# Odd layer's values taken head by head beside their queries and keys, its gates later, and a signal for every 256 columns of a weight's low part

## The chip, the cores and the metric

One Trainium2 chip, one of its NeuronCores. The metric is the device time of one execution of the whole program in microseconds (us). The work is in float32: the two operands of every large product are each split into a high part that TensorE takes in its fast format and a low remainder, and a product is three passes (high by high, low by high, high by low).

## What is computed

Two small transformer blocks one after the other, on 512 tokens of 1024 features. The first has an "even" layer (sliding-window and chunked attention) and an "odd" layer (differential attention). The second has a state-space mixer, a latent attention and two feed-forward networks. The change touches the odd layer and the splitting of all weights. The odd layer is, cut:

```python
h = rms_norm(x, norm_g)
q, k, v, gate = jnp.split(h @ w_in, [C_QK, 2 * C_QK, 2 * C_QK + C_W], axis=-1)   # 4 x 1024 columns
q = rms_norm(q.reshape(b, s, C_HEADS, 2, HEAD_DIM), qn)                # 8 heads, 2 x 64 each
k = rms_norm(k.reshape(b, s, C_HEADS, 2, HEAD_DIM), kn)
q1, q2, k1, k2 = ...                                                   # rope on each half
v = v.reshape(b, s, C_HEADS, C_V_DIM)                                  # 8 heads of 128
o = differential_attention(q1, q2, k1, k2, v, lam)                     # softmax 1 - lam * softmax 2, times v
o = rms_norm(o, subln_g) * (1.0 - lambda_init)
y = (o.reshape(b, s, C_W) * jax.nn.silu(gate)) @ w_out
return x + y
```

## The kernel before, in words

**Tiles.** Activations lie feature by feature: 8 tiles of 128 features by 512 tokens, each as a high and a low copy (`xh`, `xl`). A weight is a piece of 128 x 1024 numbers (512 KB, eight 128 x 128 blocks). For each one SP loads it into one of three `stage` buffers, ACT copies it into `wh` (step `w_hi`, one instruction, L2005), POOL subtracts that from the original into `wl` (step `w_lo`, four instructions of 256 columns, L2569, of which only the last signals), and TensorE (PE) multiplies: step `mm` is one block by all 512 tokens in three passes (L1839, L1840, and L1842, which takes the low part of the weight and waits for `w_lo` of the whole weight), eight steps to an output tile. `mm_half` (L1851, L1852, L1854) is the same for 256 tokens, `mm_tok` (L1864, L1866, L1867) gives an output with tokens on the partitions. There are three `wh`/`wl` pairs, so a weight can only be split once the third weight before it is used up.

**The order of the work.** A planner (`Plan`) runs generators against lengths of its own for each step (`length`, `LENGTHS`) and writes down a fixed order of instructions for each engine. At each moment it takes the step that can start first, and of those the one of the lowest rank. Attention has rank 1 and 2, the preparation of queries and keys 4, and the stream of projections 8, so the stream fills what attention leaves of PE. On the chip the order is fixed: an instruction that is not ready holds up all behind it on its engine.

**Odd layer before.** `stream` projects: the gates 0 to 2 by halves while the norm is still being finished (`proj_border_g`), gate 3, queries and keys of head 0, then all values in two batches of four weights (`proj_tok_g`, four PSUM banks each, copied out by DVE in `v_in`, L2232), then for head 1 to 7 its queries and keys, with gates 4 to 7 beside heads 5, 6 and 7 (`Gates.beside`), then the output projection (`outputs`). The first four gates are one ACT instruction each (`gate`, Silu, L2030) between two table loads. The last four are copied out (`gate_in`, L2065) and their Silu is taken in pairs between two table loads (`gate_s`, L2069; the load is L2000). `prep` waits until gates 0 to 3 are done before it starts `qk_prep_g`: square on ACT (L2040), sums over heads on PE (`blk`, L1878, two matmul instructions), ln and exp on ACT, the scaling on DVE (L2259, it frees the projection's bank), a turn of partitions by DMA, two products on POOL (L2577, L2582), a sum on DVE (L2264), and the split into high and low (L2202, L2539). `attend` waits until all eight pieces of values are there. It then takes the heads in order, and in each four blocks of 128 queries one after the other: scores on PE (L1884), mask and minimum on DVE (L2268, L2278), two exps on ACT (L2045), reciprocal, factor and difference on DVE (L2359, L2363, L2367). Each block is then transposed on PE (`flip`, L1892), copied out (L2054 or L2294) and multiplied with the values (`pv`, L1899). `finish` normalises a head (L2060, L2307), turns it back on PE (`feat`, L1906), multiplies it with its gate (L2317) and splits it (L2011, L2227).

**Even layer.** It has one tile of values that is already taken in the new way: copied from PSUM by ACT (`va_in`, L2035), four transposes on PE (`va_t`, L1913), copied by DVE (`va_out`).

Of the kernel before, what the change touches and what calls it, by code (L numbers as in the profile page):

```python
# [8 lines left out]
F32 = mybir.dt.float32  # L9
# [82 lines left out]
PE_DEEP, DMA_DEEP, HOP, OVERLAP = 165, 2200, 36, 90  # L92
HALF = (slice(0, 256), slice(256, 512))
# [49 lines left out]
class Weight:  # L143
# [6 lines left out]
    lo: tuple = None  # L150
    used: tuple = None
    over: bool = False

# [32 lines left out]
class Plan:  # L186
# [46 lines left out]
    def ready(self, kind, o):  # L233
        if kind in ("mm", "mm_half", "mm_tok"):
            x, kk = (o[4], o[5]) if kind == "mm_tok" else (o[3], o[4])
            done = x.half[o[5]] if kind == "mm_half" else x.t
            return max(self.when([done[kk]]), self.when(o[1]), self.when(o[0].bank.freed))
        return self.when(list(o)) + HOP

    def length(self, kind, o):  # L240
        n = o[-1] if o and isinstance(o[-1], int) else 0
        if kind in ("w_hi", "w_lo"):
            return 210 + 0.82 * o[0].n if kind == "w_hi" else 100 + 2.25 * o[0].n
# [116 lines left out]
    def split_weight(self, m):  # L360
# [6 lines left out]
        w.lo = self.put("w_lo", w)  # L367
# [744 lines left out]
def odd_layer(P, x, rt, parts, freed, over):  # L1112
# [4 lines left out]
    gates = Gates(P, mem["o_sg"], over)  # L1117
    v = mem["o_v"]
    tv = []
# [14 lines left out]
    def prep(h, j, gain, key, pool):  # L1134
        u = yield from P.proj_g(x, [w[j]])
        while None in gates.t[0:4]:
            yield lambda: None not in gates.t[0:4]
        P.start(4, P.qk_prep_g(u, (P.V(gain), tgain), True, key, pool,
                               lambda dst: got.setdefault(h, {}).__setitem__(key, dst)))
        return u  # L1140

    def v_post(b, half, u):
        t = yield ("v_in", v[:, b, half * 512:(half + 1) * 512], u, over)
        u.bank.release(t)
        tv.append(t)

    def stream():
        yield from P.proj_border_g(x, [w[j] for j in range(3)], lambda j, u: P.start(4, gates.first(j, u)))
        P.start(4, gates.first(3, (yield from P.proj_g(x, [w[3]]))))
        yield from prep(0, 8, "od_qn", "q", qs)  # L1150
        yield from prep(0, 16, "od_kn", "k", ks)
        for half in range(2):
            us = []
            for r in (P.at, P.at, P.at, P.ob):
                us.append(Unit((yield from P.taken(r))))
            yield from P.proj_tok_g(x, [T["o_v"][half, j] for j in range(4)], us)
            for b in range(4):
                P.start(5, v_post(b, half, us[b]))
        for h in range(1, 8):
            yield from prep(h, 8 + h, "od_qn", "q", qs)  # L1160
            u = yield from prep(h, 16 + h, "od_kn", "k", ks)
# [32 lines left out]
    def back(h, i, g, ready, ob, mn, sm, rr, to):  # L1194
# [3 lines left out]
        t = yield ("pv", ob, i * 128, 128, [pt.ready, tv], [cols(pt.ap, b) for b in range(nb)],  # L1198
# [6 lines left out]
    def attend():  # L1205
        while len(tv) < 8:
            yield lambda: len(tv) == 8
# [1644 lines left out]
```

## Time and profile before

| | us |
|---|---|
| median of 3 runs | 2012.36 (2011.19 to 2012.7) |
| the profiled execution | 2011.72 |
| its span, first to last instruction | 2009.9 |
| PE busy | 1936.9 (96%) |
| DVE busy | 1042.4 (52%) |
| ACT busy | 990.9 (49%) |
| POOL busy | 946.4 (47%) |

The profiled execution is 0.6 us under the median of the runs and 1.8 us longer than its span. Matmuls overlap: an L1839 row of 0.39 us starts 0.23 us before the next one, and its share of PE's time is the 0.23 us. "Idle before" is time in which an engine did nothing ahead of an instruction, with what ended it. A busy share of 96% means 73 us in which PE did nothing.

### The profile page before, as it was taken

What the parts mean: (1) busy time and instruction counts of PE and PEld (TensorE: products, weight loads), DVE (VectorE), ACT (ScalarE), POOL (GpSimd) and SP (SyncE); (2) the same over time, 40 slices, a digit from 0 to 9 for tenths busy, and PEclk for the clock granted to TensorE, in tenths of its full rate; (3) what the DMA queues carried; (4) which work ended last, traced back from release to release, by engine and by line L of the source; (5) the groups of instructions that cost most, each with busy time, mean ns of one, the idle gap of its engine ahead of it and who ended that gap; (6) DMA issues with size and microseconds to landing.
All of it is one profiled execution on the core that took longest, in us unless ns stands there. A gap on an engine that the chain in (4) does not pass through costs nothing.

```text
span 2009.9 us, 26575 instructions
## 1 busy us (share of the span) xinstructions
PE 1936.9 (96%) x10008; PEld 1607.4 (80%) x10008; DVE 1042.4 (52%) x1934; ACT 990.9 (49%) x1737; POOL 946.4 (47%) x1236
## 2 busy tenths in 40 slices
PE   6999999989989999999999999999999999999997
PEld 5778888866778877777788888888878888888886
DVE  4366543378743677766736564412546574444214
ACT  5466634367743565556526444422555464444323
POOL 4542355554535444444364555555452445555553
PEclk9999999999999999999999999999999999999999
DMA  5321223331222222222132223233221223223332
GB/s 186 95 69 43 61 76 95 90 89 53 84 62 86 74 74 74 75 74 82 56 105 85 100 95 102 94 92 99 77 70 55 74 74 105 95 95 97 95 95 71
DMA packets 55200, 169.36 MB, mean 84 GB/s; under 512 B 7072, under 2 KB 13856, under 8 KB 54944
## 3 DMA queue, kind: packets, MB, share of 16 engines
q1 hardware_dynamic: 54784, 166.92, 26.5%
q8 instruction: 79, 1.29, 0.3%
q10 hardware_dynamic: 288, 0.74, 0.1%
q14 instruction: 49, 0.40, 0.1%
HBM read 158.72 MB, written 2.10 MB: 80 GB/s over the span
## 4 chain that ended last, share of the span: by engine, by line
PE 77%; DVE 12%; ACT 4%; POOL 3%; issue 2%; DMA 1%; SPq 0%; ACTq 0%; DVEq 0%; POOLq 0%
PE ps L1839 19%; PE ps L1842 19%; PE ps L1840 19%; PE ps L1899 2%; POOL wl L2569 2%; PE ps L1851 2%; PE ps L1854 2%; PE ps L1852 2%; PE ps L1884 2%; DVE tmp L2392 1%; PE ps L1892 1%; DVE s_xbc L2371 1%; PE ps L1864 1%; PE ps L1866 1%; PE ps L1867 1%
## 5 line engine op out<-in xcount | busy, mean ns | idle before, releaser
L2569 POOL TENSOR_TENSOR wl<-st,wh 128x256 fp32r<-128x256 f32 (+1 forms) x1180 | 877.2, 776 | 998.7 <-ACT wh L2005 998.2
L2005 ACT ACTIVATE wh<-st 128x1024 fp32r<-128x1024 f32 (+2 forms) x311 | 314.2, 1011 | 502.2 <-PE ps L1842 441.7
L1839 PE MATMUL ps<-xh,wh 128*128 128x512 f32 x1368 | 555.5, 406 | 1.6 <-DVE tmp L2259 1.6
L1842 PE MATMUL ps<-xh,wl 128*128 128x512 f32 x1368 | 534.3, 391 | 0.8 <-POOL wl L2569 0.8
L1840 PE MATMUL ps<-xl,wh 128*128 128x512 f32 x1368 | 533.2, 390 | 0.0
L1839 PEld LDWEIGHTS ps<-xh,wh 128*128 128x128 f32 x1368 | 257.3, 188 | 60.0 <-issue 8.3
L1842 PEld LDWEIGHTS ps<-xh,wl 128*128 128x128 f32 x1368 | 256.7, 188 | 56.9 <-POOL wl L2569 1.7
L1840 PEld LDWEIGHTS ps<-xl,wh 128*128 128x128 f32 x1368 | 257.5, 188 | 49.8 <-issue 2.6
L2526 DVE SCALAR_TENSOR_TENSOR tmp<-ps,vec,tmp 128x510 f32<-128x510 f32 (+1 forms) x176 | 131.3, 749 | 209.8 <-ACT tmp L2184 206.9
L2484 DVE SCALAR_TENSOR_TENSOR res<-res,ps 128x512 f32<-128x512 f32 (+1 forms) x37 | 22.7, 615 | 220.9 <-PE ps L1842 212.2
L1839 PE MATMUL ps<-fa_h,wh 128*128 128x512 f32 x308 | 120.6, 392 | 0.0
L1842 PE MATMUL ps<-fa_h,wl 128*128 128x512 f32 x308 | 119.9, 389 | 0.0
L1840 PE MATMUL ps<-fa_l,wh 128*128 128x512 f32 x308 | 119.8, 389 | 0.0
L1851 PE MATMUL ps<-xh,wh 128*128 128x256 f32 x288 | 86.4, 300 | 8.0 <-DVE xl L2227 5.2
L1854 PE MATMUL ps<-xh,wl 128*128 128x256 f32 x288 | 83.8, 291 | 5.7 <-POOL wl L2569 5.6
L2011 ACT ACTIVATE fa_h<-tmp 128x512 fp32r<-128x512 f32 x44 | 27.8, 632 | 116.8 <-DVE tmp L2532 116.8
L1852 PE MATMUL ps<-xl,wh 128*128 128x256 f32 x288 | 83.5, 290 | 0.0
L2371 DVE SCALAR_TENSOR_TENSOR s_xbc<-ps,vec,s_xbc 128x509 f32<-128x509 f32 (+2 forms) x96 | 71.2, 742 | 9.0 <-ACT s_xbc L2078 8.1
L2045 ACT ACTIVATE o_pr<-ps,small 128x256 f32<-128x256 f32 (+3 forms) x112 | 55.6, 501 | 28.5 <-DVE small L2278 22.2
L1840 PEld LDWEIGHTS ps<-fa_l,wh 128*128 128x128 f32 x308 | 57.8, 188 | 12.5 <-issue 0.5
L1839 PEld LDWEIGHTS ps<-fa_h,wh 128*128 128x128 f32 x308 | 57.8, 188 | 12.4 <-issue 0.5
L1842 PEld LDWEIGHTS ps<-fa_h,wl 128*128 128x128 f32 x308 | 57.8, 188 | 12.0
(276 smaller groups left out, 3508.7 us busy)
## 6 DMA issues: line engine op xcount, KB each, us to landing
st<-in_f_up SPq DMA_DIRECT2D x88, 512.0 KB, 3.2
st<-in_s_xbc SPq DMA_DIRECT2D x32, 512.0 KB, 3.5
st<-in_f_dn SPq DMA_DIRECT2D x32, 512.0 KB, 3.5
st<-in_o_fm SPq DMA_DIRECT2D x24, 512.0 KB, 3.5
st<-in_e_fm SPq DMA_DIRECT2D x21, 512.0 KB, 3.5
st<-in_s_z SPq DMA_DIRECT2D x16, 512.0 KB, 3.5
st<-in_s_out SPq DMA_DIRECT2D x16, 512.0 KB, 3.5
tmp<-tmp SPq DMA_DIRECT2D x100, 64.0 KB, 2.0
```

What stands on the lines that cost most here:

```text
L1839: e.matmul(u.bank.ap, hi, x.h[:, kk, :], start=first, stop=False)
L1840: e.matmul(u.bank.ap, hi, x.l[:, kk, :], start=False, stop=False)
L1842: e.matmul(u.bank.ap, lo, x.h[:, kk, :], start=False, stop=last).then_inc(S["mm"], 1)
L1851: e.matmul(out, hi, x.h[:, kk, part], start=first, stop=False, skip_group_check=True)
L1852: e.matmul(out, hi, x.l[:, kk, part], start=False, stop=False, skip_group_check=True)
L1854: e.matmul(out, lo, x.h[:, kk, part], start=False, stop=last, skip_group_check=True).then_inc(S["mm_half"], 1)
L1884: t = e.matmul(out, q[:, i * 128:i * 128 + 128], k[:, kb0 * 128:kb0 * 128 + n], start=(j == 0), stop=(j == len(passes) - 1))
L2005: e.activation(P.mem["wh"][w.m % NWR][:, 0:w.n], P.mem["stage"][w.m % NSTAGE][:, 0:w.n], ACT.Copy).then_inc(S["w_hi"], 1)
L2045: e.activation(p, s, ACT.Exp, bias=least, scale=-1.0, accum_out=total).then_inc(S["exp"], 1)
L2371: e.scalar_tensor_tensor(v[:, sh:], u.bank.ap[:, 0:SEQ - sh], weight, v[:, sh:], ALU.mult, ALU.add).then_inc(S["tap"], 1)
L2526: e.scalar_tensor_tensor(a.ap[:, sh:], u.bank.ap[:, 0:SEQ - sh], weight, a.ap[:, sh:], ALU.mult, ALU.add).then_inc(S["ftap"], 1)
L2569: t = e.tensor_tensor(P.mem["wl"][w.m % NWR][:, part], P.mem["stage"][w.m % NSTAGE][:, part], P.mem["wh"][w.m % NWR][:, part].bitcast(F32) ...
```

## The change

Four things, in the order of the diff. The low part of a weight is planned and signalled in pieces of 256 columns (`LOW`), each a step of its own, and a matmul waits for the pieces that its block lies in (`Weight.low`): blocks 0 and 1 for the first, 2 and 3 for the second and so on. The planner's length for it goes from 2404 ns for a whole weight to four times 713 ns. In the odd layer the border takes queries, keys and values of head 0, no longer three gates, and `prep` no longer waits for gates. Each head's values are a projection of their own behind its keys, brought into place by `va_in`, `va_t` and `va_out`, and `attend` waits for the values of its own head alone. The gates are all beside heads: two beside head 1, two beside 3, one beside 5, one beside 6, two beside 7, all by `gate_in` and `gate_s`. The layout of the value weights on the host follows.

```diff
+LOW = 256
@@ class Weight
+    def low(self, k, n=128):
+        return self.lo[k * n // LOW:(k * n + n - 1) // LOW + 1]
@@ Plan.ready
-            return max(self.when([done[kk]]), self.when(o[1]), self.when(o[0].bank.freed))
+            low = o[1].low(o[2], o[3]) if kind == "mm_tok" else o[1].low(o[2])
+            return max(self.when([done[kk]]), self.when([o[1].hi, low]), self.when(o[0].bank.freed))
@@ Plan.length
-            return 210 + 0.82 * o[0].n if kind == "w_hi" else 100 + 2.25 * o[0].n
+            return 210 + 0.82 * o[0].n if kind == "w_hi" else 150 + 2.2 * (o[1].stop - o[1].start)
@@ Plan.split_weight
-        w.lo = self.put("w_lo", w)
+        w.lo = [self.put("w_lo", w, slice(at, min(at + LOW, w.n))) for at in range(0, w.n, LOW)]
@@ odd_layer
+    gates.beside = {1: [0, 1], 3: [2, 3], 5: [4], 6: [5], 7: [6, 7]}
-    tv = []
+    tv = [None] * 8
-    def prep(h, j, gain, key, pool):
-        u = yield from P.proj_g(x, [w[j]])
-        while None in gates.t[0:4]:
-            yield lambda: None not in gates.t[0:4]
+    def prep(h, key, u):
+        gain, pool = ("od_qn", qs) if key == "q" else ("od_kn", ks)
         P.start(4, P.qk_prep_g(u, (P.V(gain), tgain), True, key, pool,
                                lambda dst: got.setdefault(h, {}).__setitem__(key, dst)))
-    def v_post(b, half, u):
-        t = yield ("v_in", v[:, b, half * 512:(half + 1) * 512], u, over)
+    def v_post(h, u):
+        vf = yield from P.taken(P.tmp)
+        t = yield ("va_in", vf, u)
         u.bank.release(t)
-        tv.append(t)
+        bank = yield from P.taken(P.aux)
+        t = yield ("va_t", bank, vf, t)
+        vf.release(t)
+        tv[h] = yield ("va_out", v[:, :, h * 128:(h + 1) * 128], bank, [t, over])
+        bank.release(tv[h])
+    def first(j, u):
+        if j < 2:
+            prep(0, "qk"[j], u)
+        else:
+            P.start(4, v_post(0, u))
     def stream():
-        yield from P.proj_border_g(x, [w[j] for j in range(3)], lambda j, u: P.start(4, gates.first(j, u)))
-        P.start(4, gates.first(3, (yield from P.proj_g(x, [w[3]]))))
-        yield from prep(0, 8, "od_qn", "q", qs)
-        yield from prep(0, 16, "od_kn", "k", ks)
-        for half in range(2):
-            ...
-            yield from P.proj_tok_g(x, [T["o_v"][half, j] for j in range(4)], us)
-            for b in range(4):
-                P.start(5, v_post(b, half, us[b]))
+        yield from P.proj_border_g(x, [w[8], w[16], w[24]], first)
         for h in range(1, 8):
-            yield from prep(h, 8 + h, "od_qn", "q", qs)
-            u = yield from prep(h, 16 + h, "od_kn", "k", ks)
+            prep(h, "q", (yield from P.proj_g(x, [w[8 + h]])))
+            prep(h, "k", (yield from P.proj_g(x, [w[16 + h]])))
+            P.start(4, v_post(h, (yield from P.proj_g(x, [w[24 + h]]))))
             for j in gates.beside.get(h, ()):
                 u = yield from P.proj_g(x, [w[j]])
                 P.start(5, gates.bring(j, u))
@@ odd_layer back, attend
-        t = yield ("pv", ob, i * 128, 128, [pt.ready, tv], ...
+        t = yield ("pv", ob, i * 128, 128, [pt.ready, tv[h]], ...
-        while len(tv) < 8:
-            yield lambda: len(tv) == 8
-            while len(got.get(h, ())) < 2:
+            while len(got.get(h, ())) < 2 or tv[h] is None:
@@ pe_program, mm, mm_half and (with n) mm_tok
-            pe.wait_ge(w.lo)
+            pe.wait_ge(w.low(k))
@@ pool_program
-            w, = o
+            w, part = o
             pool.wait_ge(w.hi)
-            for at in range(0, w.n, 256):
-                part = slice(at, min(at + 256, w.n))
-                t = e.tensor_tensor(...)
-            t.then_inc(S["w_lo"], 1)
+            e.tensor_tensor(...).then_inc(S["w_lo"], 1)
```

## Rows read from the trace of the kernel before

**Rows 1.** The page: busy time, and PE and its clock in 40 slices.
```profile
PE 1936.9 (96%) x10008; PEld 1607.4 (80%) x10008; DVE 1042.4 (52%) x1934; ACT 990.9 (49%) x1737; POOL 946.4 (47%) x1236
PE   6999999989989999999999999999999999999997
PEclk9999999999999999999999999999999999999999
```
**Rows 2.** Busy time in stretches of the odd layer, engine by engine.
```profile
core 0: us, PE busy (x) PEld busy (x) DVE busy (x) ACT busy (x) POOL busy (x), PEclk, DMA share, GB/s
318.00:380.20 62.20, 62.20 (x273) 50.76 (x272) 13.37 (x16) 21.76 (x27) 38.40 (x51) 1.00 0.36 112
380.20:397.50 17.30, 16.99 (x85) 13.41 (x83) 9.59 (x23) 9.56 (x24) 6.92 (x9) 1.00 0.33 100
440.00:461.00 21.00, 19.52 (x102) 15.25 (x102) 16.02 (x34) 15.21 (x42) 9.72 (x12) 1.00 0.23 70
557.00:575.50 18.50, 17.35 (x91) 14.24 (x89) 10.21 (x27) 12.12 (x34) 2.83 (x4) 1.00 0.15 56
575.50:590.30 14.80, 10.77 (x46) 8.16 (x45) 5.90 (x10) 7.23 (x18) 3.31 (x5) 0.88 0.00 1
320.00:580.00 260.00, 243.42 (x1175) 190.99 (x1174) 152.26 (x288) 155.20 (x365) 133.11 (x152) 1.00 0.27 80
```
**Rows 3.** Waits of PE, 395 to 582 us: line, for whom, total, times, longest.
```profile
PE ps L1892 <- DVE o_pr L2367: 9.3, 15, 1.9
PE ps L1899 <- DVE o_pt L2294: 2.0, 3, 1.0
PE ps L1899 <- ACT o_pt L2054: 1.7, 2, 1.1
PE ps L1839 <- DVE tmp L2259: 1.6, 2, 1.1
PE ps L1884 <- DVE kz L2539: 1.4, 1, 1.4
PE ps L1906 <- DVE tmp L2307: 0.5, 2, 0.3
```
**Rows 4.** Timeline of PE at heads 0, 1, 6 and 7: start, duration.
```profile
380.19 0.56 PE L1884 MATMUL ps<-kz,qz 128*128 128x128 f32 x4
397.51 0.66 PE L1892 MATMUL ps<-const,o_pr 128*128 128x128 f32 x4 [0.32 <-DVE o_pr L2367]
...
405.55 1.08 PE L1878 MATMUL ps<-tmp,const 128*128 128x512 f32 x2
417.94 0.63 PE L1884 MATMUL ps<-kz,qz 128*128 128x128 f32 x4 [1.35 <-DVE kz L2539]
...
554.20 0.66 PE L1892 MATMUL ps<-const,o_pr 128*128 128x128 f32 x4 [1.93 <-DVE o_pr L2367]
554.61 0.47 PE L1839 MATMUL ps<-xh,wh 128*128 128x512 f32 x1
575.53 0.66 PE L1892 MATMUL ps<-const,o_pr 128*128 128x128 f32 x4
```
**Rows 5.** Waits of PE for the low part of a weight, whole span.
```profile
PE ps L1854 <- POOL wl L2569: 5.6, 3, 2.3
PE ps L1842 <- POOL wl L2569: 2.5, 3, 1.6
```
**Rows 6.** Timeline at one such wait: POOL's four pieces, PE's matmuls.
```profile
17.66 3.54 POOL L2569 TENSOR_TENSOR wl<-st,wh 128x256 fp32r<-128x256 f32 x4 [1.46 <-ACT wh L2005]
...
18.53 0.41 PE L1852 MATMUL ps<-xl,wh 128*128 128x256 f32 x1
21.25 0.58 PE L1854 MATMUL ps<-xh,wl 128*128 128x256 f32 x1 [2.31 <-POOL wl L2569]
```
**Rows 7.** Timeline of PE at the end of the odd layer's attention.
```profile
584.28 0.62 PE L1839 MATMUL ps<-yh,wh 128*128 128x512 f32 x1 [2.23 <-DVE yl L2227]
585.55 0.63 PE L1839 MATMUL ps<-yh,wh 128*128 128x512 f32 x1
590.30 0.50 PE L1842 MATMUL ps<-yh,wl 128*128 128x512 f32 x1 [1.63 <-POOL wl L2569]
```
**Rows 8.** Timeline around the even layer's one tile of values (L1913 `va_t`).
```profile
67.05 0.57 ACT L2035 ACTIVATE tmp<-ps 128x512 f32<-128x512 f32 x1
67.68 0.66 PE L1913 MATMUL ps<-const,tmp 128*128 128x128 f32 x4 [1.22 <-ACT tmp L2035]
68.09 0.48 PE L1864 MATMUL ps<-wh,xh 128*128 128x512 f32 x1
68.40 0.39 PE L1866 MATMUL ps<-wl,xh 128*128 128x512 f32 x1
68.64 0.39 PE L1867 MATMUL ps<-wh,xl 128*128 128x512 f32 x1
```
**Rows 9.** Timeline of PE across the start of an output tile (323.33).
```profile
322.65 0.39 PE L1839 MATMUL ps<-xh,wh 128*128 128x512 f32 x1
323.33 0.39 PE L1839 MATMUL ps<-xh,wh 128*128 128x512 f32 x1
324.01 0.39 PE L1839 MATMUL ps<-xh,wh 128*128 128x512 f32 x1
```
**Rows 10.** Timeline of ACT at one pair of gates.
```profile
523.25 1.28 ACT L2000 ACT_TABLE_LOAD   x1
524.55 1.15 ACT L2069 ACTIVATE sg<-sg 128x512 f32<-128x512 f32 x2
525.72 1.28 ACT L2000 ACT_TABLE_LOAD   x1
527.01 0.63 ACT L2011 ACTIVATE yh<-tmp 128x512 fp32r<-128x512 f32 x1
```
**Rows 11.** Groups of DVE and POOL instructions: busy, mean ns.
```profile
L2363 DVE SCALAR_TENSOR_TENSOR small<-small,small,lam 128x1 f32<-128x1 f32 x32 | 12.3, 384 | 1.0
L2367 DVE SCALAR_TENSOR_TENSOR o_pr<-o_pr,small,o_pr 128x512 f32<-128x512 f32 x8 | 7.3, 917 | 0.3
L2569 POOL TENSOR_TENSOR wl<-st,wh 128x256 fp32r<-128x256 f32 x127 | 95.1, 782 | 103.0 <-ACT wh L2005 103.0
```

More of the change, by code:

```diff
@@ L149 @@
     hi: tuple = None
-    lo: tuple = None
+    lo: list = None
     used: tuple = None
     over: bool = False
+    def low(self, k, n=128):
+        return self.lo[k * n // LOW:(k * n + n - 1) // LOW + 1]
 @dataclass
@@ L1197, in back @@
         g.p_uses[0].release(t)
-        t = yield ("pv", ob, i * 128, 128, [pt.ready, tv], [cols(pt.ap, b) for b in range(nb)],
+        t = yield ("pv", ob, i * 128, 128, [pt.ready, tv[h]], [cols(pt.ap, b) for b in range(nb)],
                    [v[:, b, h * 128:(h + 1) * 128] for b in range(nb)])
@@ L1205, in attend @@
     def attend():
-        while len(tv) < 8:
-            yield lambda: len(tv) == 8
         for h in range(8):
-            while len(got.get(h, ())) < 2:
-                yield lambda: len(got.get(h, ())) == 2
+            while len(got.get(h, ())) < 2 or tv[h] is None:
+                yield lambda: len(got.get(h, ())) == 2 and tv[h] is not None
             q, k = got[h]["q"], got[h]["k"]
@@ L1852, in pe_program @@
             e.matmul(out, hi, x.l[:, kk, part], start=False, stop=False, skip_group_check=True)
-            pe.wait_ge(w.lo)
+            pe.wait_ge(w.low(k))
             e.matmul(out, lo, x.h[:, kk, part], start=False, stop=last,
@@ L1864, in pe_program @@
             e.matmul(out, x.h[:, kk, toks], hi, start=first, stop=False)
-            pe.wait_ge(w.lo)
+            pe.wait_ge(w.low(k, n))
             e.matmul(out, x.h[:, kk, toks], lo, start=False, stop=False)
@@ L2564, in pool_program @@
         if kind == "w_lo":
-            w, = o
+            w, part = o
             pool.wait_ge(w.hi)
-            for at in range(0, w.n, 256):
-                part = slice(at, min(at + 256, w.n))
-                t = e.tensor_tensor(P.mem["wl"][w.m % NWR][:, part], P.mem["stage"][w.m % NSTAGE][:, part],
-                                    P.mem["wh"][w.m % NWR][:, part].bitcast(F32), ALU.subtract)
-            t.then_inc(S["w_lo"], 1)
+            e.tensor_tensor(P.mem["wl"][w.m % NWR][:, part], P.mem["stage"][w.m % NSTAGE][:, part],
+                            P.mem["wh"][w.m % NWR][:, part].bitcast(F32), ALU.subtract).then_inc(S["w_lo"], 1)
         elif kind == "rope_c":
@@ L2798, in layouts @@
     r["e_out"] = fm(e_out)
-    r["o_fm"] = fm(cat([o[:, 3072:4096], o[:, 0:2048]], 1))
-    r["o_v"] = tm(o[:, 2048:3072], 2)
+    r["o_fm"] = fm(cat([o[:, 3072:4096], o[:, 0:3072]], 1))
     r["o_out"] = fm(i["od_w_out"][0])
```

4 lines of the change are left out of this document (removed).

## The prediction

> **What bounds the kernel now.** I read the page first. PE is busy 96% of the span at a granted clock in its highest tenth, and no other engine passes 52% [rows 1]. So only two things can move the time: what PE is given to do, and the 73 us in which it does nothing (2009.9 - 1936.9). The dips in its row of tenths lie at the start, in slices 9 to 12 (402 to 603 us, the odd layer's attention) and at the ends of layers. The stretches of the odd layer show where [rows 2]. From 318 to 380 us, all projection, PE has no idle time at all. From 320 to 580 us it has 260.0 - 243.4 = 16.6 us, nearly all after attention begins at 380. The end, 575.5 to 590.3 us, has 4.0 us more at a clock of 0.88.
>
> Next comes who PE waited for in the attention [rows 3]: six rows, 16.5 us, and 9.3 of them are flips that wait for the DVE difference `mix_d` ahead of them. The timeline shows their form [rows 4]: at 554.20 PE waits 1.93 us for a flip, and 0.41 us later it goes on with projection. Work of the stream was there during the wait; the fixed order had the flip first. The planner gives the factor (`mix_c`) 160 ns and the 512-wide difference 160 + 1.04 x 512 = 692 ns, and the rows have 384 and 917 [rows 11]. So attention comes later than PE's order expects, by 0.45 us in such a block from these two alone. This matters for the whole forecast: most of the 16.5 us is no lack of work for PE, and giving it more work beside attention doesn't by itself remove it.
>
> How much PE waits goes with how crowded DVE and ACT are. Head 0 (380.2 to 397.5 us) has DVE busy 9.59 of 17.3 us (55%) and PE idle 0.3 us; head 7 has 10.21 of 18.5 (55%) and 1.15 us; head 2, with other heads' queries and keys prepared beside it, has 16.02 of 21.0 (76%) and 1.5 us [rows 2]. The two light heads together have 1.5 us, so the six others have 16.5 - 1.5 = 15 us, or 2.5 each (all between 397.5 and 557 us).
>
> **Part 1, values by heads and attention earlier: the waits.** PE's projections stay: 8 value weights of 24 matmuls each before, 8 tiles of 24 after, 0.23 us apart in either form. Three tiles cover the border instead of three gates, so no work is lost there. What moves is when attention starts: now at 380.19 us, after the values [rows 4]. The new border ends near 318 us, and from the last `blk` of a key to its first score head 1 took 417.94 - 405.55 = 12.4 us [rows 4], to which I add 2 us for the square ahead of it and `blk` itself: attention can start near 332 us. Eight heads at 17.3 to 21.8 us each need about 170 us, and they now have some 240. PE needs more per head than the chain does: three tiles and on average one gate, 4 x 8 x 3 x 0.2275 = 21.8 us, and about 8 us of attention and `blk`, so 30 us against 21. The heads will come when their projections come, with pauses between them. Inside a head the order is as tight as before, so its waits stay in kind. They shrink with the crowd. In a 21 us head two thirds of the next head's preparation fall beside it instead of all of it: DVE then has its own 10 us and two thirds of some 7, or 70% busy, which is between 55% (0.75 us a head) and 80% (2.5 us). I take 1.7 us a head, 13.5 us in all: **-3 us**. Ends: -10 (all heads as light as heads 0 and 7, 8 x 0.8) and +1.
>
> A new wait can appear at each head's start. Head 1 is the one head before whose scores followed directly on its preparation, and PE waited 1.35 us for its keys [rows 3, 4]. Now seven heads do so. The planner's pace for POOL gets truer in the same change (2852 ns for a whole low part, where four pieces of 782 take 3128 [rows 11], in place of 2404), and products of the rope are queued behind such parts. So I hold this at zero beyond the 1.7 us a head, with seven times 1.35 = +9.5 us as the upper end.
>
> **Part 2, the transposes.** The only new work of PE. In the even layer the four of `va_t` start at 67.68 us and the second matmul behind them at 68.40, 0.72 us for what takes 0.23 without them: 0.49 us [rows 8]. Eight times that is 3.9 us, all on the engine that bounds. The same row has a wait of 1.22 us for ACT's copy, once. Per head that is between 0 and 1.22 us; I take 0.2 because the planner's 620 ns for this copy is above the row's 570, so its lateness comes from the ACT queue alone: 1.6 us. Together **+5.5 us**, ends 3.9 and 13.7.
>
> The Trainium skill ("TensorE: Matmul & The Clock Gate", Part 4: PE-mode transpose) gives about 275 ns for one transpose in a kernel's context. The trace has the same as a duration, but four overlap and take PE's time for 0.49 us. By the page's figure, taken one after another, 32 transposes would be an estimated 8.8 us instead of 3.9, and the sum 4.9 us longer.
>
> **Part 3, copies and gates on the side engines.** DVE: eight `v_in` become eight `va_out` of the same size, nothing. ACT: eight copies of 0.57 us [rows 8] are new, four gates of one instruction become two (4 x 0.58 us more [rows 10]), and three pairs of table loads become four: two loads of 1.28 us [rows 10]. Together 4.6 + 2.3 + 2.6 = 9.5 us on ACT, which has 105 us free from 320 to 580 us (260.0 - 155.2) [rows 2]. Cost on the path zero as long as attention has pauses between heads; a pair of gates does hold ACT for 3.8 us (523.25 to 527.01), and two more such blocks now lie beside exps. That is inside the upper ends above. Nothing is added for DMA: the value weights are the same size, and SP's queue of loads and turns has the same entries.
>
> The Trainium skill ("ScalarE: Activation LUTs", What ACT_TABLE_LOAD costs) puts a switch at 1283 ns and a drain of about 1380 more. The trace has the 1.28, and the Silu starts 0.02 us behind it, so no drain shows here [rows 10]. With the page's figure the two extra loads would be an estimated 5.3 us of ACT, and the sum unchanged.
>
> **Part 4, the low part in pieces.** PE waits for it six times in the whole kernel, 5.6 + 2.5 = 8.1 us [rows 5]. At one of them POOL runs four pieces from 17.66 to 21.20 us and PE's third pass, due at 18.94, starts at 21.25 [rows 6]. It needed only the first piece, which ends near 18.5: the wait goes. So it is at 590.30 (1.63 us) [rows 7]. Afterwards PE takes 1.37 us for two blocks of 512 tokens (6 x 0.2275) and POOL 0.78 for the next piece, so PE doesn't catch up; in halves it is 0.72 against 0.78, which can give back some tenths three times. What is late next at the layer borders is the low half of the activations, from DVE. I take **-5 us**; ends -8.1 and -1. The price: about three more waits on PE per weight. At 323.33 us PE starts a new tile, with waits on its bank and weight already fulfilled, and its step is 0.68 us like the two beside it [rows 9]: zero. POOL signals four times instead of once per weight, with no more instructions: zero. New planner lengths can also shuffle the order elsewhere, where I see no direction: up to 2 us either way.
>
> **Part 5, the end.** PE idles 2.23 us for the last head's split, and then nine matmuls run 0.43 us apart instead of 0.23 (584.28 to 585.55 for three), the lower of the two clock levels, which follows that idle time (the stretch has 0.88) [rows 7, 2]: 4.0 us. After, behind head 7's keys come its values, gates 6 and 7 and 21 steps of the output projection: 5.5 + 10.9 + 14.3 us, with head 7's and 6's own 9 or 10 some 40 us. Against it stands a chain of 14 (preparation) + 18.5 (head 7) + 8.75 (575.53 to 584.28) = 41 us [rows 4, 7]. They are even, where before values were not among the fillers. I take half: **-2 us**, ends -4 and +4.
>
> **The sum,** against the profiled execution: 2011.7 - 3 + 5.5 - 5 - 2 = 2007.2. The profiled execution is 0.6 us under the median of the runs, so 2007 to 2008; I say **2007**.
>
> **Rivals.** (a) *Attention's waits vanish.* With attention 48 us earlier, all heads run like 0 and 7. For it: those two heads, and 70 us of room in the chain. Against it: the waits come from planner lengths that the change leaves alone. -10 in place of -3, the end -4, transposes 3.9, low parts -5: 2011.7 - 15.1 = 1997. (b) *Slower: each head starts on the heels of its preparation.* The chain has room, so each of heads 1 to 7 has its first scores placed where the planner thinks its keys are ready, and PE stands still there for 1.35 us as at head 1. For it: that row. Against: the truer POOL length. It decides once a preparation that takes 12.4 us on the chip is planned 1.35 us shorter, as head 1's wait says it was. +9.5 in place of -3 and no gain at the end: 2011.7 + 9.5 + 5.5 - 5 = 2022. (c) *The low parts gain nothing,* because DVE's halves are late next at the borders and the order is planned tighter against POOL: -1 in place of -5, the rest as forecast: 2011. This is also the case in which that half of the change doesn't do what it says.
>
> **Chances.** Forecast 0.38, (a) 0.18, (b) 0.26, (c) 0.18. The measurement can tell about 0.2%, or 4 us: faster is under 2008.3, slower above 2016.4. The forecast's own range is 2001 to 2013; two thirds of it count as faster. With (a) and a little of (c): faster 0.46. (b) less a little, with a little of (c): slower 0.26. The rest, 0.28, is the same. The range for 8 in 10 goes from 1996, just past (a), to 2020, which leaves out half of (b).
>
> **What would show it.** Right: first scores near 332 us; waits of PE for the low part below 3 us in all; flips waiting for `mix_d` 6 to 8 us; L1913 with 36 matmuls and little idle time; PE busy about 4 us more. (a) would have the waits for `mix_d` under 3 us; (b) a row of L1884 waiting for keys seven times; (c) rows of L1851 for the low half of the activations that grow by what L1854 loses. Wrong altogether: a stretch in which PE has no projection to do, for instance since temporaries or banks run out with preparations waiting for a free set of query and key tiles.

## The result

The changed kernel takes 2002.3 us (median of 4 runs, 2000.55 to 2003.19) against 2012.5 in the same comparison. The ratio of the runs is 0.9944, with an interval of 0.9932 to 0.9957: 11.3 us or 0.6% faster (8.7 to 13.7), where the two medians are 10.2 us apart. I had said 2007, in a range of 1996 to 2020. The time and its side are inside the forecast, the gain is 2.5 times the 4.5 us of its sum.

The profiled execution has a span of 1998.7 us, 11.2 less than before. The page after, the lines that answer to [rows 1]:

```profile
PE 1934.7 (97%) x10040; PEld 1609.2 (81%) x10040; DVE 1043.1 (52%) x1942; ACT 995.8 (50%) x1743; POOL 948.8 (47%) x1236
PE   6999999999999999999999999999999999999997
PEclk9999999999999999999999999999999999999999
```

The dips in slices 9 to 12 are gone. PE has 32 matmul instructions more and yet 2.2 us less busy time. Some of what counted as busy before was matmuls at the lower clock: nine of them at the end of attention alone, 1.8 us more than at the higher [rows 7]. The rest of that difference isn't accounted for. Idle time fell from 73 to 64 us.

To say where, I cut the span at the first half-width matmul of each layer's output projection, which is at 280.96, 602.43, 1041.1, 1404.97, 1603.64 and 1969.3 us after the change. The first stretch starts with the program; its first projection starts at 16.98 (before: 16.87).

| stretch | before, us | after, us | difference |
|---|---|---|---|
| start and even layer | 284.41 | 280.96 | -3.5 |
| odd layer | 327.35 | 321.47 | -5.9 |
| state-space mixer | 438.70 | 438.67 | 0.0 |
| first feed-forward | 364.58 | 363.87 | -0.7 |
| latent attention | 199.76 | 198.67 | -1.1 |
| second feed-forward | 365.68 | 365.66 | 0.0 |

PE's waits after, between 320 and 575 us, which answer to [rows 3] (line, for whom, total, times, longest; L1896 is the flip, L1903 `pv`, L1882 `blk`, L1917 `va_t`, L1888 the scores, L1843 the first pass of a projection):

```profile
PE ps L1896 <- DVE o_pr L2371: 5.1, 9, 0.9
PE ps L1843 <- DVE tmp L2263: 2.7, 2, 1.5
PE ps L1903 <- DVE o_pt L2298: 1.3, 2, 0.7
PE ps L1882 <- ACT tmp L2044: 1.2, 2, 0.6
PE ps L1917 <- ACT tmp L2039: 0.8, 2, 0.4
PE ps L1888 <- ACT kz L2206: 0.6, 1, 0.6
PE ps L1888 <- DVE kz L2543: 0.2, 1, 0.2
```

They sum to 11.9 us where [rows 3] have 16.5. Waits for the low part are gone from the whole span; what took their place at the borders is the low half of the activations, in the list of PE's waits over the whole span:

```profile
PE ps L1855 <- DVE xl L2231: 7.1, 6, 4.8
PE ps L1855 <- DVE xl L2508: 2.6, 4, 1.8
```

Those two were 5.2 and 2.3 us before, so 2.2 of the 8.1 us [rows 5] came back there.

Two places of PE's timeline after the change (start, length, instruction; in brackets the idle time before it). The first scores, and the end of attention, which answers to [rows 7]:

```profile
332.08 0.63 PE L1888 MATMUL ps<-kz,qz 128*128 128x128 f32 x4 [0.18 <-DVE kz L2543]
...
575.16 0.60 PE L1910 MATMUL ps<-const,tmp 128*128 128x128 f32 x4
577.99 0.50 PE L1843 MATMUL ps<-yh,wh 128*128 128x512 f32 x1 [2.23 <-DVE yl L2231]
578.33 0.39 PE L1844 MATMUL ps<-yl,wh 128*128 128x512 f32 x1
578.56 0.39 PE L1846 MATMUL ps<-yh,wl 128*128 128x512 f32 x1
```

The 2.23 us for the last head's split are still there, to the hundredth. But the matmuls behind it go on 0.23 us apart, where before nine of them were 0.43 apart, and no wait for a low part follows.

### The profile page after: what moved, and what is told of

It is laid out like the page before. It is cut to its first block, busy times and chain, and to the rows that moved or that the text cites. A ratio compares the mean times of both kernels' runs of the same rounds, so it can differ in the third digit from the quotient of the medians.

```text
span 1998.7 us, 26979 instructions
## 1 busy us (share of the span) xinstructions
PE 1934.7 (97%) x10040; PEld 1609.2 (81%) x10040; DVE 1043.1 (52%) x1942; ACT 995.8 (50%) x1743; POOL 948.8 (47%) x1236
## 4 chain that ended last, share of the span: by engine, by line
PE 79%; DVE 12%; ACT 3%; issue 2%; POOL 2%; DMA 1%; SPq 0%; ACTq 0%; DVEq 0%; POOLq 0%
PE ps L1843 20%; PE ps L1846 20%; PE ps L1844 20%; PE ps L1903 3%; PE ps L1888 3%; PE ps L1855 2%; PE ps L1858 2%; PE ps L1856 2%; PE ps L1896 1%; DVE tmp L2396 1%; POOL wl L2571 1%; DVE s_xbc L2375 1%; PE ps L1877 1%; DVE s_st L2412 1%; DVE tmp L2419 1%
## 5 line engine op out<-in xcount | busy, mean ns | idle before, releaser
L1843 PE MATMUL ps<-xh,wh 128*128 128x512 f32 x1432 | 584.8, 408 | 3.5 <-DVE tmp L2263 3.5
L1846 PE MATMUL ps<-xh,wl 128*128 128x512 f32 x1432 | 559.2, 390 | 0.0
L1844 PE MATMUL ps<-xl,wh 128*128 128x512 f32 x1432 | 558.2, 390 | 0.0
L1843 PEld LDWEIGHTS ps<-xh,wh 128*128 128x128 f32 x1432 | 269.4, 188 | 64.2 <-issue 10.4
L1846 PEld LDWEIGHTS ps<-xh,wl 128*128 128x128 f32 x1432 | 268.7, 188 | 57.9
L1844 PEld LDWEIGHTS ps<-xl,wh 128*128 128x128 f32 x1432 | 269.6, 188 | 54.2 <-issue 4.8
L1843 PE MATMUL ps<-fa_h,wh 128*128 128x512 f32 x308 | 120.6, 392 | 0.0
L1855 PEld LDWEIGHTS ps<-xh,wh 128*128 128x128 f32 x288 | 56.5, 196 | 14.9 <-DVE xl L2231 9.4
L1843 PEld LDWEIGHTS ps<-fa_h,wh 128*128 128x128 f32 x308 | 57.8, 188 | 12.5 <-issue 0.5
L1844 PEld LDWEIGHTS ps<-fa_l,wh 128*128 128x128 f32 x308 | 57.8, 188 | 12.5 <-issue 0.5
```

The lines of the kernel that those rows point to most:

```text
L1843: e.matmul(u.bank.ap, hi, x.h[:, kk, :], start=first, stop=False)
L1844: e.matmul(u.bank.ap, hi, x.l[:, kk, :], start=False, stop=False)
L1846: e.matmul(u.bank.ap, lo, x.h[:, kk, :], start=False, stop=last).then_inc(S["mm"], 1)
L1855: e.matmul(out, hi, x.h[:, kk, part], start=first, stop=False, skip_group_check=True)
```

## The experiments

All times are medians; "against before" is the ratio of the runs, with its 95% interval, and the us are that ratio times 2012.5. The kernel before was run again in each comparison, with medians from 2012.5 to 2014.9, so a time is to be compared by its ratio. "Odd layer" is the stretch defined above in the one profiled execution, with PE's idle time in it.

| kernel | odd layer | signals | planner | time | against before | us | odd layer stretch, idle |
|---|---|---|---|---|---|---|---|
| before | old | whole | old | | 1 | 0 | 327.4, 22.6 |
| lo_only | old | pieces | new | 2008.4 | 0.9977 (0.9968 to 0.9986) | -4.6 | 327.0, 20.1 |
| signal_only | old | pieces | old | 2009.3 | 0.9983 (0.9974 to 0.9992) | -3.4 | 324.9, 20.5 |
| odd_only | new | whole | old | 2017.3 | 1.0023 (1.0014 to 1.0031) | +4.6 | 333.0, 22.3 |
| odd_signal | new | pieces | old | 2010.9 | 0.9981 (0.9972 to 0.9990) | -3.8 | 328.4, 19.6 |
| odd_planner | new | whole | new | 2015.8 | 1.0006 (0.9997 to 1.0015) | +1.2 | 327.4, 20.3 |
| piece_601 | new | pieces | new, 601 ns | 2005.9 | 0.9964 (0.9952 to 0.9976) | -7.2 | 324.8, 18.9 |
| after | new | pieces | new | 2002.3 | 0.9944 (0.9932 to 0.9957) | -11.3 | 321.5, 16.3 |
| gates_first | new, gates ahead | pieces | new | 2001.3 | 0.9943 (0.9931 to 0.9956) | -11.5 | 320.6, 14.9 |
| twice_vat | new | pieces | new | 2005.7 | 0.9953 (0.9941 to 0.9966) | -9.5 | 323.1, 14.7 |
| mix_len | new | pieces | new, 2 lengths | 1996.3 | 0.9909 (0.9894 to 0.9924) | -18.3 | 314.8, 11.7 |
| mix_old | old | pieces | new, 2 lengths | 2000.0 | 0.9932 (0.9920 to 0.9944) | -13.7 | 320.1, 17.5 |
| true_all | new | pieces | new, more lengths | 1992.3 | 0.9895 (0.9880 to 0.9910) | -21.1 | 313.5, 10.2 |
| true_old | old | pieces | new, more lengths | 2001.3 | 0.9940 (0.9926 to 0.9953) | -12.1 | 320.1, 15.7 |

### The parts alone

**lo_only**: the kernel before with `LOW`, the pieces, their waits and the planner's part. **odd_only**: the kernel before with the odd layer's part alone.

> The low part in pieces of 256 columns alone, signals and planner together; the odd layer as in the kernel before. Theory A (the parts add up; waits for the low part are worth nearly all their 8.1 us, and the odd layer's part the rest): 7 us under before, no wait of PE for the low part over 0.5 us in all, the even layer 3 to 4 us shorter, the odd layer 3. Theory B (the whole gain comes from the values by heads; behind the low part the halves of the activations are late): 1 to 2 us under before, and the row of L1855 waiting for DVE grows by what the row of the third pass loses.

> The odd layer's part alone: values by heads, gates beside heads; the low part signalled once per weight and planned as before. Theory A: 4 us under before, six waits for the low part of 8 us in all as before. Theory B: 9 to 10 us under before. Theory C (the parts help each other: the planner's truer length for POOL is what makes just-in-time preparations come in time): 0 to 2 us under before, with new waits of scores for keys and of projections for banks that the kernel after doesn't have.

Measured: -4.6 and +4.6 us. They sum to nothing, and together they are 11.3 us faster. None of the three theories had odd_only slower by that much; the one that the parts help each other is nearest. Where odd_only loses is in its timeline. At the border of the odd layer, and behind the last head (L1837, L1838 and L1840 are the three passes here):

```profile
301.56 0.38 PE L1852 MATMUL ps<-xh,wl 128*128 128x256 f32 x1 [1.43 <-POOL wl L2567]
...
584.88 0.66 PE L1904 MATMUL ps<-const,tmp 128*128 128x128 f32 x4 [0.86 <-DVE tmp L2305]
587.76 0.50 PE L1837 MATMUL ps<-yh,wh 128*128 128x512 f32 x1 [2.23 <-DVE yl L2225]
...
593.72 0.80 PE L1840 MATMUL ps<-yh,wl 128*128 128x512 f32 x1 [2.98 <-POOL wl L2567]
594.31 0.63 PE L1837 MATMUL ps<-yh,wh 128*128 128x512 f32 x1
594.74 0.63 PE L1838 MATMUL ps<-yl,wh 128*128 128x512 f32 x1
595.17 0.63 PE L1840 MATMUL ps<-yh,wl 128*128 128x512 f32 x1
...
599.43 0.50 PE L1837 MATMUL ps<-yh,wh 128*128 128x512 f32 x1
```

Three idle times in a row, the last for a whole low part, and then 13 matmuls 0.43 us apart until 599.4, where 0.23 is the pace of the higher clock: 2.98 + 13 x 0.20 = 5.6 us for one wait. The same stretch of odd_only by windows of 4 us, with the columns of [rows 2] (sum, then busy time and count of PE, PEld, DVE, ACT and POOL, then PEclk, DMA share and GB/s):

```profile
592.00:596.00 4.00, 2.28 (x5) 1.82 (x6) 1.93 (x2) 1.34 (x2) 4.00 (x5) 0.60 0.26 71
596.00:600.00 4.00, 4.00 (x12) 3.12 (x10) 0.00 (x0) 0.00 (x0) 3.63 (x6) 0.54 0.57 192
```

So a wait at a layer's end may cost up to twice its length. But not all of the 13 need belong to this wait. odd_signal, below, has the same order of instructions and no wait for a low part there, and has eight matmuls at the lower pace all the same:

```profile
586.92 0.50 PE L1842 MATMUL ps<-yh,wh 128*128 128x512 f32 x1 [2.23 <-DVE yl L2230]
587.25 0.39 PE L1843 MATMUL ps<-yl,wh 128*128 128x512 f32 x1
...
588.80 0.63 PE L1843 MATMUL ps<-yl,wh 128*128 128x512 f32 x1
589.23 0.63 PE L1845 MATMUL ps<-yh,wl 128*128 128x512 f32 x1
```

The Trainium skill ("TensorE: Matmul & The Clock Gate", Part 1) has two levels too, 1.2 and 2.4 GHz; the rows here show the price, 0.20 us for each matmul of 512 columns.

### Signals against the planner's order

**signal_only** and **odd_signal** are lo_only and the kernel after with the planner as before, so that in signal_only each engine's steps stand in the very order of the kernel before:

```diff
-            return max(self.when([done[kk]]), self.when([o[1].hi, low]), self.when(o[0].bank.freed))
+            return max(self.when([done[kk]]), self.when(o[1]), self.when(o[0].bank.freed))
-            ... 150 + 2.2 * (o[1].stop - o[1].start)
+            ... (100 + 2.25 * o[0].n) * (o[1].stop - o[1].start) / o[0].n
```

**odd_planner** is the reverse, the kernel after with `pe.wait_ge(w.lo)` in all three kinds of matmul. **piece_601** has only the second of the two edits above.

> As the low part in pieces, but the planner keeps its length for a whole low part and its rule that a matmul needs all of it, so that the order of all instructions is that of the kernel before; only signals and waits are in pieces. If the gain of the pieces is that PE stops waiting, this has it: 5 to 7 us under before. If it comes from the new order, this has 1 to 2 us and the run with the planner's part the rest.

> The odd layer's change with signals and waits in pieces, but the order of all instructions that of the run odd_only (the planner keeps its length for a whole low part and its rule that a matmul needs all of it). Theory A (what the odd layer's change alone loses are stops of PE for the low part at the border and behind the last head, 1.4 and 3.0 us, each with a stretch at the lower clock behind it): 7 to 8 us under odd_only, so some 2 to 3 under before. Theory B (it is the planner's order that the two parts need each other for): 3 us under odd_only, as the signals alone gave in the old odd layer, so about 2 us above before.

> The kernel after in its own order of instructions, but each matmul waits for the whole low part. Theory A: the stops return (1.4 us at a border, up to 3 behind the last head, 2.3 at the start), 6 to 9 us slower than the kernel after, near 2009. Theory B: within 3 us of the kernel after, near 2004.

> The kernel after with the planner's length for a piece of the low part at 601 ns, a quarter of the old 2404, in place of 713; a matmul is still planned on its own piece. It lies between odd_signal (old length, planned on the whole) and the kernel after, which are 7.5 us apart. If the length is what counts (preparations queued on POOL behind low parts are planned too early): 5 us or more slower than the kernel after. If being planned on the piece is what counts: within 2 us of the kernel after.

With the old odd layer the signals give 3.4 us, less than the 5 to 7 I expected of them although all waits for low parts are gone. The profile tells why: 8.1 us of them went, and PE's waits for `xl` grew from 7.5 to 11.3 us. The planner's part adds 1.2, within the noise. With the new odd layer they give 8.4 us (+4.6 to -3.8), as theory A of odd_signal had it, though from a higher start; and the planner's part then gives another 7.5 (-3.8 to -11.3), which theory A didn't have. piece_601 splits these 7.5 into about 3.5 for planning a matmul on its own piece and 4.0 for the length of 713 instead of 601 ns, each with an uncertainty of about 3, so the split isn't shown. Taking the signals out of the finished kernel costs 12.5 us (odd_planner), four times what theory B allowed and more than the 6 to 9 of theory A. Here the waits account for it. In the same order as the kernel after, PE waits 13.1 us for low parts and 2.1 less for `xl`, 11.0 us together. The longest is again at the layer's end, and matmuls at the lower pace stand behind it, where the kernel after has neither:

```profile
586.97 0.47 PE L1846 MATMUL ps<-yh,wl 128*128 128x512 f32 x1 [3.07 <-POOL wl L2571]
...
588.10 0.63 PE L1846 MATMUL ps<-yh,wl 128*128 128x512 f32 x1
588.52 0.63 PE L1843 MATMUL ps<-yh,wh 128*128 128x512 f32 x1
```

PE's waits in the odd layer of odd_signal, the six largest groups (L1895 flip, L1842 first pass, L1854 first pass of a half, L1887 scores, L1881 `blk`), show what the truer order changes:

```profile
PE ps L1895 <- DVE o_pr L2370: 6.9, 12, 1.4
PE ps L1842 <- DVE yl L2230: 2.2, 1, 2.2
PE ps L1854 <- DVE xl L2230: 1.9, 2, 1.7
PE ps L1842 <- DVE tmp L2262: 1.9, 3, 1.1
PE ps L1887 <- DVE kz L2542: 1.5, 3, 0.9
PE ps L1881 <- ACT tmp L2043: 1.5, 3, 0.6
```

Waits of scores for keys are 1.5 us here and 0.8 after (0.6 for ACT's part, 0.2 for DVE's), flips 6.9 and 5.1; the layer's idle time is 3.3 us more than after's. Of the 3.6 us that are left between the two stretches, the clock has the larger part: in odd_signal 12 half-width matmuls run at the lower pace from 301.8 to 305.1 and eight full ones from 588.4 to 591.8 us, an estimated 2.7 us (12 x 0.09 and 8 x 0.20), in the kernel after at neither place.

### The granted clock beside the planner's part

Every execution was measured with its mean granted clock, as a share of the full one. Averaged over the executions of a kernel:

| | old odd layer | new odd layer |
|---|---|---|
| whole signals, old lengths | 0.9936 to 0.9941 | 0.9937 |
| pieces, old lengths (signal_only, odd_signal) | 0.9953 | 0.9946 |
| pieces, lengths of the change (lo_only, after) | 0.9925 | 0.9958 |
| and factor and difference (mix_old, mix_len) | 0.9950 | 0.9958 |
| and five more (true_old, true_all) | 0.9922 | 0.9960 |

A mean that is 0.001 lower can cost PE at most 2.0 us of 2007, an estimate for the case that PE works through all of that time at half the pace (0.43 us apart in place of 0.23). Between executions of one kernel 0.001 goes with 1.0 us, an estimate from 158 executions. So the 6.3 us by which the planner's part is worth more with the new odd layer (7.5 less 1.2) stand beside a difference of 0.0040, an estimated 4 to 8 us. That difference alone may be what keeps the two edits from adding. In the profile of lo_only three stretches of the odd layer are at the lower level, behind idle times of 3.1, 1.4 and 2.2 us; in that of the kernel after there is none:

```profile
534.40:541.20 6.80, 5.62 (x14) 4.01 (x15) 4.05 (x9) 3.04 (x9) 4.12 (x5) 0.50 0.53 151
571.95:575.35 3.40, 3.40 (x11) 2.63 (x10) 1.13 (x3) 0.16 (x2) 0.00 (x0) 0.50 0.02 5
585.60:589.00 3.40, 3.40 (x10) 2.62 (x9) 2.63 (x4) 3.40 (x5) 2.54 (x4) 0.50 0.00 0
```

No run holds the clock fixed, so how much of the 6.3 us it is stays open, as does what in an order brings such stretches.

### The gates' place and the transposes

**gates_first** undoes "no gates ahead"; **twice_vat** does every four transposes of values twice.

```diff
-        yield from P.proj_border_g(x, [w[8], w[16], w[24]], first)
-        for h in range(1, 8):
+        yield from P.proj_border_g(x, [w[j] for j in range(3)], lambda j, u: P.start(4, gates.first(j, u)))
+        P.start(4, gates.first(3, (yield from P.proj_g(x, [w[3]]))))
+        for h in range(8):
@@ twice_vat
-            for i in range(4):
-                t = e.transpose(cols(bank.ap, i), cols(vf.ap, i), ident)
+            for i in range(8):
+                t = e.transpose(cols(bank.ap, i % 4), cols(vf.ap, i % 4), ident)
```

> The kernel after with four gates ahead again (three in the border, one behind), and queries, keys and values of head 0 behind them; gates 4 to 7 beside heads 5, 6 and 7. It undoes 'no gates ahead' alone: one pair of table loads and four instructions of ACT less, attention some 22 us later. If the gates' place matters little: within 2 us of the kernel after. If late gates buy the gain as work for PE beside attention: 4 us or more slower than the kernel after, with more waits of flips. If their table loads beside the exps cost something: 1 to 3 us faster than the kernel after.

> The kernel after with each head's four transposes of values done twice, and the even layer's four too (9 x 4 more transposes; the planner doesn't know). By the rows of before 0.45 us for four of them: +4.0 us against the kernel after. If waits of PE hide them: under 1. If each took its 275 ns alone: +9.9.

The gates' place is worth nothing: 0.9943 against 0.9944. Attention that starts some 17 us later and two table loads less make no difference that shows. The doubled transposes cost 1.8 us (ratios 0.9953 and 0.9944, each +-0.0013, so between nothing and 5.4) where their work is 4.0, which the times alone don't rule out. In the profile the odd layer is 1.6 us longer and its idle time 1.6 us shorter, so about half of the added work filled waits of PE in that one execution. The 275 ns of a transpose taken one after another, an estimated 9.9 us more, is ruled out.

### The planner's lengths

**mix_len** is the kernel after with two lengths changed, **mix_old** is lo_only with the same; **true_all** and **true_old** have these and five more.

```diff
-    "mix_c": 160
+    "mix_c": 384
+        if kind == "mix_d":
+            return 480 + 0.9 * n
@@ true_all and true_old besides
+    "mask": 165, "rope_add": 990, pool 1390 (1280), a piece of the low part 780 ns (713)
+        if kind == "head_lo":
+            return 300 + 1.04 * n
```

> The kernel after with two of the planner's lengths set to what the rows of before have: the factor 384 ns in place of 160, the difference 480 + 0.9 n (941 ns at 512 columns) in place of 160 + 1.04 n. If flips wait because the order is planned for a shorter chain: the 5.1 us of PE waiting for that difference fall under 2, and the time by 3 to 4 us. If they wait because DVE and ACT are crowded: those waits stay within 1 us, and so does the time.

> The low part in pieces, the odd layer as in the kernel before, and the planner's two lengths for factor and difference as in the run mix_len. Theory A (the truer lengths are worth 7 us wherever attention is planned, and values by heads stay worth 6 to 7 on top): 7 us under lo_only, near 2001, and still 5 to 7 us slower than mix_len. Theory B (values by heads gained because they gave slack to an order planned too tight, so that truer lengths give the same thing by themselves): 10 us or more under lo_only, within 2 us of mix_len.

> As mix_len, with more of the planner's lengths set near the rows: the products of the rope 1390 ns (planned 1280), their sum 990 (692), the low halves of queries and keys 832 (692), a piece of the low part 780 (713), the mask 165 (112). If true lengths keep paying: 2 to 4 us under mix_len, with PE's waits for banks, for keys and for the difference together 3 us or less. If what is left comes from durations that vary with POOL's work and no fixed length can meet: within 2 us of mix_len.

> The low part in pieces, the odd layer as in the kernel before, and all the planner's lengths of the run true_all. Theory A (values by heads are worth something of their own under a planner with true lengths, 7 us as with wrong ones): near 1999. Theory B (they are worth some 4 us, as between mix_old and mix_len; the rest of their gain was slack for an order planned too tight): near 1996. Theory C (nothing of their own): within 2 us of true_all, 1991 to 1994.

Two numbers in the planner give 7.0 us on the kernel after (0.9944 to 0.9909), at the same mean clock of 0.9958. On lo_only they give 9, with the mean clock 0.0025 higher, an estimated 2.5 to 5 us of it. mix_old is 4.6 us behind mix_len, between its two theories. I had expected 3 to 4 us of mix_len, and the waits of flips to fall under 2 us. The time is better than that and the waits are not. Three of PE's largest groups of waits in the odd layer of mix_len (L1898 flip, L1845 first pass) and of true_all (L1900 flip, L1847 first pass):

```profile
PE ps L1898 <- DVE o_pr L2373: 4.6, 6, 1.5
PE ps L1845 <- DVE tmp L2265: 2.0, 2, 1.2
PE ps L1845 <- DVE yl L2233: 1.5, 1, 1.5
```

```profile
PE ps L1900 <- DVE o_pr L2375: 2.6, 4, 1.7
PE ps L1847 <- DVE yl L2235: 2.2, 1, 2.2
PE ps L1847 <- DVE tmp L2267: 1.0, 2, 0.8
```

They are fewer (6 and 4 in place of 9 after and 15 before) and it is the sum over all kinds that falls, the layer's idle time from 16.3 to 11.7 and 10.2 us. A truer length for two steps moves everything planned behind them. true_all is 1.4 per thousand below mix_len, which two intervals of 1.5 can't separate. Its waits for banks, keys and the difference are 5.3 us together (1.0, 1.7 and 2.6), where I had 3 or less. In its profile the even layer's stretch is 261.2 us, 2.8 less than after's 264.0, with 1.6 us of idle time in place of 4.9, and the odd layer's 1.3 less than mix_len's.

The same kernels, read in pairs, give what the new odd layer is worth:

| what the planner has | old odd layer | new odd layer | new less old, us |
|---|---|---|---|
| whole signals, old lengths | 1 | 1.0023 | +4.6 |
| pieces, old lengths | 0.9983 | 0.9981 | -0.4 |
| pieces, lengths of the change | 0.9977 | 0.9944 | -6.6 |
| and factor and difference | 0.9932 | 0.9909 | -4.6 |
| and five more | 0.9940 | 0.9895 | -9.1 |

The same edit is 4.6 us slower, nothing, or up to 9 us faster. For true_old I had said 1999 if the odd layer keeps its own worth and 1996 if part of it had been slack: 2001.3 is on the side of its own worth. But the clock's table has the same pairs: by it an estimated 3 us or all of the 6.6, 1 to 2 of the 4.6 and 4 to 8 of the 9.1 us may be the granted clock. The last three differences are each uncertain by 3 to 4 us besides, so no order among them is shown.

true_all is the fastest kernel of the study: 1992.3 us, 0.9895 of before, and 0.9895 / 0.9944 = 0.995 of the kernel after.

## Why the prediction was right, and where it was not

**What bounds the kernel** held. PE is at 97%, nothing happened where little of its time was idle (the mixer and the second feed-forward are equal to 0.03 us), and 9.3 of the profile's 11.2 us lie in the even and the odd layer. That the time fell into the range is in part luck: two errors of the sum, told under the low part, have opposite signs.

**Attention's start and pauses** held. The first scores came at 332.08, forecast near 332. That the waits inside a head stay in kind, since the order and not the lack of work makes them, was right, and mix_len and mix_old show it from outside: two planner lengths are worth 7 us with the new odd layer and 9 with the old. Rival (a), waits that vanish with the crowd, fell: 11.9 us of 16.5 remain. The time could not have told: by the ratio, 2001 lies nearer to (a)'s 1997 than to 2007. I had put 13.5 + 1.6 us against these 11.9. The 13.5 rested on a loose reading, 80% of DVE and 2.5 us of waits for a crowded head, where the row of head 2 has 76% and 1.5. The wait for `mix_d` is 5.1 us, a little under the 6 to 8 I named.

**Rival (b)**, heads on the heels of their preparation, did not come with the change, 0.8 us in all for keys instead of 9.5. It had its seed: with the old planner length those waits were 1.5 us, in odd_signal and in piece_601. So the reason I gave for holding it at zero, the truer length for POOL, was right in sign, and piece_601 gives the length alone 4.0 us, between nothing and 7.5. But I had used it only to cancel a loss, not as a gain.

**The transposes** were taken at 5.5 us with their waits. Twice_vat puts their work at about 1.8, and the rows have 0.8 us of waits for the odd layer's eight: some 3 us too much. That is by the middle of an interval from nothing to 5.4. As far as it goes, the step that failed is "all on the engine that bounds": where PE waits every few microseconds anyway, part of new work that is ready goes into those waits. The estimate by the figure of the Trainium skill ("TensorE: Matmul & The Clock Gate", Part 4: PE-mode transpose), 8.8 us for the transposes alone, was further off.

**The low part in pieces** was taken at -5 us and measures -4.6 alone. This term was right where it was measured by itself, and wrong as a term of a sum. The sum's own form was the step that failed: odd layer +0.5 and pieces -5 added to -4.5. Measured it is +4.6 and -4.6 alone and -11.3 together. I had costed the odd layer on the waits for low parts of the old order, 1.43 and 1.63 us. In the new order without pieces they are 1.43 and 2.98, the second behind two other waits and followed by 5.7 us at the lower clock; and the pieces gain more in the new layer (8.4 us) than in the old (3.4). And the planner's own part of that edit, which I had called a shuffle "where I see no direction: up to 2 us either way", is worth 1.2 us with the old odd layer and 7.5 with the new, with the clock's share of that open. In the terms of the sum, the odd layer was 4.1 us dearer than forecast (+4.6 for +0.5) and the pieces behind it gave 15.9 in place of 5; the difference, 6.8 us, is the error.

One reading of the rows was off: at 0.21 us a matmul the third pass was due near 18.75, not at 18.94. signal_only has it at 18.80, so the wait went as forecast.

**The end of attention.** I took half of 4.0 us. The 2.23 us stayed and the stretch at the lower clock behind it went (about 1.8 us): right in size, for the wrong half, and so by luck. gates_first, as fast as the kernel after, has such a stretch of six matmuls behind the same 2.23 us, so its absence isn't shown to be the change's doing. That fillers would cover the chain was wrong; the last split is waited for as long as before.

**PE's busy time** was forecast 4 us up and fell 2.2. Busy time contains matmuls at the lower clock; PE's busy time is no measure of its work when their share changes.

**Rival (c)** holds in part: of 8.1 us of waits 2.2 came back as waits for `xl`, and in signal_only, whose order is that of the kernel before, 3.8 did: 4.3 us are left of them, and 3.4 were measured. At its first border nothing at all is left of the 2.3 us saved: waits for `xl` of 0.7 and 0.3 us are new, matmuls run at the lower pace from 17.3 to 19.6 and again from 23.5 to 26.5 us, and the step behind them starts at 26.70, before at 26.58.

**The even layer and what is left open.** The even layer's 3.5 us belong to the planner's part. Counted from the first matmul of its border, the stretch takes 266.3 to 267.5 us in the four kernels with the old planner (before, signal_only, odd_only, odd_signal) and 263.8 to 265.1 in those with the new one (lo_only, odd_planner, piece_601, after, gates_first, twice_vat), whatever their signals. How much of it is order and how much clock isn't told apart. Nor was it tried why stretches at the lower clock come behind some idle times and not others: 2.23 us before 577.99 had none behind it, the same 2.23 before 584.28 had one, and in odd_signal it came 1.5 us later.

## What to carry to other kernels

When a fixed order is written by a planner, two edits that each meet it needn't add: cost the second in the order that the first makes, or measure all four corners; here one corner was 4.6 us slower and the far one 11.3 faster. Read the mean granted clock beside each corner too, since it can differ by as much as the effect. Compare the planner's lengths with the trace's durations before restructuring the work: two of them, 160 against 384 ns and 692 against 917, were worth 7 to 9 us, about as much as the new layer in its best pair. And signal a producer's pieces as they are done wherever a consumer needs the first piece only, above all at layer ends, where matmuls at the lower clock can follow a wait.

## What the runs showed of the hardware

A stop of PE at a layer's end can cost more than its length: behind the 2.98 us in odd_only, 13 matmuls ran 0.43 us apart instead of 0.23, and behind the 3.07 us in odd_planner eight; the kernel after, in the same order as the latter, has neither the stop nor such matmuls. The clock's column doesn't always show such a stretch: between 20 and 24 us of the kernel before half-width matmuls start 0.21 us apart, which is the pace of the lower level (0.12 is that of the higher), and the column reads 1.00.

A wait that is already fulfilled costs PE nothing that shows: the second feed-forward has the same length to 0.02 us with four waits for the low part of each weight as with one.

A DVE sum of two operands in SBUF has no fixed length: in the kernel after one and the same form of the rope's sum takes 666 to 1769 ns. The first row is the view of that one line between 316 and 580 us (least, median and most in ns), the second the groups of DVE's instructions by form in the same stretch (busy us, mean ns, idle before):

```profile
L2268 DVE TENSOR_TENSOR tmp<-tmp,tmp x16: 666/924/1769, 321.5 to 545.1; 128x512 f32<-128x512 f32 x16
L2268 DVE TENSOR_TENSOR tmp<-tmp,tmp 128x512 f32<-128x512 f32 x16 | 17.1, 1069 | 19.8 <-POOL tmp L2583 19.7
```

The timelines of DVE and POOL tell the two kinds apart. Of these 16 sums, the seven with no POOL instruction beside them took 666 to 693 ns. Of the nine with one beside them (a piece of a low part, or the product of the rope), eight took 1155 to 1769 ns and one 694. The Trainium skill ("GPSIMD Engine Reference", 8. Key points) says that POOL shares its SBUF interfaces with VectorE and contends with instructions of two SBUF inputs; but for the one of 694 ns, the rows agree. POOL's own spans are rough, and no run changed only what POOL does then. The spread bounds what a planner with one length for a step can reach.
